# Position-bias rows written to memory once instead of 128 times, and another order of the first loads, in a four-layer encoder trunk

## Chip, cores and metric

One core of a Trainium2 chip runs the whole program. The metric is device microseconds of one execution, the median of the runs; three runs were taken of the kernel before.

## What is computed

Four post-norm layers run over 256 tokens of width 1024. Layers 0 and 3 mix tokens by differential attention with a shared relative-position bias, layer 1 by a gated linear recurrence, layer 2 by a short convolution. Each layer also attends to 256 memory tokens and ends with a gated feed-forward block. The part that the change touches is the bias of the attention layers, one number for each pair of positions and each of 6 heads, taken from a table of 32 buckets:

```python
bias = table[_t5_bucket(k_pos[None, :] - q_pos[:, None])].transpose(2, 0, 1)
logits = jnp.einsum('bqhmd,bkhmd->bmhqk', qb, k).astype(jnp.float32) + bias
probs = jax.nn.softmax(logits, axis=-1)
w = (probs[:, 0] - lam * probs[:, 1]).astype(v.dtype)
```

The bias depends on key position minus query position alone, so one row of 512 numbers for each head holds all of it.

## The kernel before

**Weights.** All weights lie in one stream in memory, cut into 404 units of 128 partitions x 4 KB (512 KB each), in the order of use. Unit u goes through four steps on four engines: SyncE issues its load into one of RAW = 5 buffers (line 473); ScalarE rounds it to a high part (line 784, "hi u" below); VectorE subtracts to get the low part (line 976, "lo u"); TensorE multiplies with both parts, three matmuls for each pair of tiles (lines 572 to 574, 584 to 588, 599 to 601). The high and low parts have SPLIT = 5 buffers of their own, so "hi u" waits until TensorE is done with unit u - 5 (`unit_done`), and the load of unit u waits for "lo" of unit u - 5 (`lo_ready`). A chunk is two units; a "half" is TensorE's work on one unit.

**Order.** `make_schedule` writes one list of items, and each engine walks it in order and does its own part of each item. At the head of the list stand: the turn (transposition) of the input tokens; chunk 0 (units 0 and 1, the query of the memory attention, "XQ"); `bias_rows`; the turn of the first 128 memory tokens ("turn mem 0"); chunk 1 (units 2 and 3, head 0's query and key, with "turn mem 1" between its halves); chunk 2 (units 4 and 5, keys of the memory, "KM"); chunk 3 (units 6 and 7, values of the memory) with the first memory logits "xlog 0" between its halves; then "xexp 0" (their exponentials on ScalarE, line 898) and `prepare` (small tables made ready on VectorE, which waits for all of `small_landed`); chunk 4 (units 8 and 9, head 1) with "xlog 1" between its halves; then "log 0", the first logits of the position-bias attention (line 668). While TensorE is on unit u, ScalarE and VectorE split unit u + 4. "log 0" uses the same PSUM banks as "xlog 0" and waits until "xexp 0" has read them.

**Bias.** TensorE multiplies the table with a one-hot matrix (line 649), ScalarE copies the resulting 6 x 512 rows from PSUM to `bias_rows` in SBUF (line 886, `rows_ready`). SyncE then writes them to `scratch` in memory once for each of 128 partitions (line 507, 1536 KB, `rows_out`), with a row pitch that makes a skewed reading possible, and reads them back skewed as `bias` (128 partitions x 6 heads x 384, line 491, 1152 KB, `bias_landed`), so that partition p holds the row shifted by p. This reading is done twice, for layer 0 and, later, for layer 3. VectorE adds the bias to the logits and takes the row maximum in one instruction (line 1177), 4 for each head.

**SyncE's queue.** All loads are issued by SyncE, one after the other, and a wait there holds all that stands behind it. The order at the start is: tokens, identity, units 0 to 2, one-hot matrix and table, memory tokens (`y_tok`, 1024 KB), units 3 and 4, eight small tables (the seven of `small[2:]` and `lam_w`), then units 5, 6, ... each after its `lo_ready`. The wait for `rows_ready` and the scratch write stand behind unit 9 (`u == RAW + 4`), the wait for `rows_out` and the bias load behind unit 13 (`u == RAW + 8`).

Of the kernel before, what the change touches and what calls it, by code (L numbers as in the profile page):

```python
# [25 lines left out]
P = 128  # L26
SEQ = 256
# [5 lines left out]
HEADS = MIX // P  # L33
# [4 lines left out]
HD = 64  # L38
# [9 lines left out]
RAW, SPLIT, AHEAD = 5, 5, 4  # L48
LEVELS = 8

ALU = mybir.AluOpType
ACT = mybir.ActivationFunctionType
F32 = mybir.dt.float32
# [127 lines left out]
def trunk_kernel(nc, stream, x, mem, rel_bias, ln, ln_cols, lam, subln, lower, hnorm, cconv, fconv,  # L181
# [38 lines left out]
    for pos, item in enumerate(items):  # L220
# [15 lines left out]
        if name == "hpv" or (name == "pv" and item[2] % 2 == 0):  # L236
            p = item[2] if name == "hpv" else item[2] // 2
# [6 lines left out]
    with ExitStack() as ctx:  # L244
        def sb(name, shape, dt=F32):
            return ctx.enter_context(nc.sbuf_tensor(name, shape, dt))

        def sem(name):
            return ctx.enter_context(nc.semaphore(name))
# [42 lines left out]
        row_max = sb("row_max", [P, 2, 4])  # L292
# [9 lines left out]
        with ExitStack() as place:  # L302
            def here(name, shape, dt=F32):
                return place.enter_context(nc.sbuf_tensor(name, shape, dt))
# [9 lines left out]
        with ExitStack() as place:  # L314
# [10 lines left out]
            bias = here("bias", [P, HEADS, 384])  # L325
            onehot = here("onehot", [NB, 512])
            table = here("table", [NB, HEADS])
            bias_rows = here("bias_rows", [HEADS, 512])
            masks_in = here("masks_in", [P, LEVELS, P])
            lam_w = here("lam_w", [P, 2, 4, HD])  # L330
# [26 lines left out]
        def head_sq(layer, p):  # L357
# [7 lines left out]
        table_landed, small_landed, bias_landed, rows_out = sem("table_landed"), sem("small_landed"), sem("bias_landed"), sem("rows_out")  # L365
# [22 lines left out]
        h_ready, prod_ready, gb_read = sem("h_ready"), sem("prod_ready"), sem("gb_read")  # L388
        dve_step, pool_step = sem("dve_step"), sem("pool_step")

        scratch = nc.dram_tensor("bias_scratch", [P, HEADS, 512], F32, kind="Internal").ap()
        out_dram = out.rearrange("b (t p) d -> p (b t) d", p=P)
        x_dram = x.rearrange("b (t p) d -> p (b t) d", p=P)
        mem_dram = mem.rearrange("b (t p) d -> p (b t) d", p=P)
        small = [(onehot, onehot_c), (table, rel_bias), (ln_col, ln_cols), (masks_in, masks_c), (fconv_w, fconv),
                 (cconv_w, cconv), (hnorm_w, hnorm), (subln_w, subln), (lower_w, lower)]
        SMALL = 16 * (len(small) - 2 + 1)

        def first_of(layer, roles):
            return next(c for c, ch in enumerate(chunks) if ch[2] == layer and ch[1] in roles)  # L400
# [58 lines left out]
        def side_bank(pos, k=0):  # L459
            return SIDE[side_ord[pos, k][0]]  # L460
# [4 lines left out]
        @block.sync  # L465
        def _(sp):
            for t in range(TT):
                sp.dma_start(x_tok[:, t], x_dram[:, t]).then_inc(x_landed[t], 16)
                if t == 0:
                    sp.dma_start(ident[:], ident_c).then_inc(ident_landed, 16)  # L470

            def load_unit(u):
                sp.dma_start(raw[:, u % RAW, :], stream[u // 2, :, (u % 2) * UNIT:(u % 2 + 1) * UNIT]).then_inc(
                    raw_landed[u % RAW], 16)

            load_unit(0)
            load_unit(1)
            load_unit(2)
            for dst, src in small[:2]:
                sp.dma_start(dst[:], src).then_inc(table_landed, 16)  # L480
            sp.dma_start(y_tok[:], mem_dram).then_inc(mem_landed, 16)
            for u in range(3, RAW):
                load_unit(u)
            for dst, src in small[2:]:
                sp.dma_start(dst[:], src).then_inc(small_landed, 16)
            sp.dma_start(lam_w[:], bass.AP(tensor=lam.tensor, offset=0, ap=[[0, P], [1, 2 * 4 * HD]])).then_inc(
                small_landed, 16)

            def load_bias():

                sp.dma_start(bias[:], bass.AP(tensor=scratch.tensor, offset=127,
                                              ap=[[HEADS * 512 - 1, P], [512, HEADS], [1, 384]])).then_inc(bias_landed, 16)

            for u in range(RAW, 2 * nchunks):
                c = u // 2
                sp.wait_ge(lo_ready, u - RAW + 1)
                load_unit(u)
                if u % 2 == 0 and c in load_gains:
                    m = load_gains[c]
                    if m >= 1:  # L500
                        sp.wait_ge(x_ready, TT * m)
                    sp.dma_start(gains[:], bass.AP(tensor=ln.tensor, offset=m * 2 * D,
                                                   ap=[[0, P], [1, 2 * D]])).then_inc(gains_landed, 16)
                if u == RAW + 4:

                    sp.wait_ge(rows_ready, 1)
                    sp.dma_start(scratch.rearrange("p h i -> h p i"),
                                 bias_rows[:].rearrange("h (one i) -> h one i", one=1).broadcast_to([HEADS, P, 512])).then_inc(rows_out, 16)
                if u == RAW + 8:
                    sp.wait_ge(rows_out, 16)  # L510
                    load_bias()
                if u == 2 * first_of(2, ("CG",)) + 16:
                    sp.wait_ge(x_ready, TT * 4)
                    load_bias()
            for t in range(TT):

                sp.wait_ge(*((x_ready, TT * (2 * DEPTH - 1) + 1) if t == 0 else (out_ready, 1)))
                sp.dma_start(out_dram[:, t], x_tok[:, t]).then_inc(out_landed, 16)
            sp.wait_ge(out_landed, 16 * TT)
# [441 lines left out]
        def _(dve):  # L961
# [3 lines left out]
            def link(ins):  # L965

                steps[0] += 1
                ins.then_inc(dve_step, 1)
                dve.wait_ge(dve_step, steps[0])
# [27 lines left out]
            def two(ap):  # L997
                return ap.rearrange("p (a s) -> p a s", a=2)
# [97 lines left out]
            for pos, item in enumerate(items):  # L1096
# [7 lines left out]
                elif name == "turn" and item[1] not in ("x", "mem"):  # L1104
                    m, t, n = item[1], item[2], ordinal[pos]
                    for b in range(2):
                        at = (slice(None), slice(4 * b, 4 * b + 4), slice(t * P, (t + 1) * P))
# [15 lines left out]
                elif name == "turn":  # L1123
                    what, t = item[1], item[2]
                    n = ordinal[pos]
                    hi, lo = (memT_hi, memT_lo) if what == "mem" else (xT_hi, xT_lo)
                    for b in range(2):
                        at = (slice(None), slice(4 * b, 4 * b + 4), slice(t * P, (t + 1) * P))
# [3 lines left out]
                elif name == "stats":  # L1132
# [4 lines left out]
                    for h in range(2):  # L1137
                        at = slice(h * 512, (h + 1) * 512)
# [25 lines left out]
                elif name in ("xlog", "log"):  # L1164
                    n = logit_ord[pos]
                    s = n % 2
                    dve.wait_ge(logits_done, n + 1)
                    if name == "xlog":
                        for i in range(2):
                            last = v.tensor_reduce(row_max[:, s, 2 * i:2 * i + 2], two(ACC[2 * s + i][:]), AX, ALU.max)  # L1170
                    else:
                        if n == head_logit[0] or n == head_logit[HEADS]:
                            dve.wait_ge(bias_landed, 16 if n == head_logit[0] else 32)
                        for i in range(2):
                            for t in range(TT):
                                j, at = 2 * i + t, (1 - t) * P
                                last = v.tensor_tensor_reduce(
                                    lg[:, s, i, t, :], ACC[2 * s + i][:, t * SEQ:(t + 1) * SEQ],
                                    bias[:, item[2], at:at + SEQ], 1.0, -3.0e38, ALU.add, ALU.max, row_max[:, s, j:j + 1])
                    link(last)  # L1180
                    v.tensor_scalar(neg_max[:, s, :], row_max[:, s, :], -1.0, None, ALU.mult).then_inc(max_ready, 1)
                elif name in ("xprob", "prob"):
                    n = prob_ord[pos]
                    s = n % 2
# [27 lines left out]
                elif name == "ms":  # L1212
                    p = item[2]
# [3 lines left out]
                elif name == "scale":  # L1217
                    layer, p = item[1:]
# [4 lines left out]
                    for i in range(2):  # L1223
                        s = slice(i * SEQ, (i + 1) * SEQ)
                        h = 2 * p + i
# [8 lines left out]
                elif name == "level":  # L1234
                    p, n = item[2], item[3]
# [3 lines left out]
                    if n < LEVELS:  # L1239
                        dst, src = DG[:, p].rearrange("p i k s -> p (i k s)"), side_bank(pos)[:]  # L1240
# [86 lines left out]
def shape_constants():  # L1327


    half, exact = NB // 2, NB // 4  # L1330
    rel = np.arange(-SEQ + 1, SEQ + 1)
    n = np.abs(rel)
    nf = np.maximum(n, 1).astype(np.float32)
    large = exact + (np.log(nf / np.float32(exact)) / np.float32(math.log(MAXD / exact))
                     * np.float32(half - exact)).astype(np.int32)
    bucket = np.where(rel > 0, half, 0) + np.where(n < exact, n, np.minimum(large, half - 1))
    onehot = (bucket[None, :] == np.arange(NB)[:, None]).astype(np.float32)
    s, t = np.arange(P)[:, None], np.arange(P)[None, :]
    masks = np.zeros((P, LEVELS, P), np.float32)
    masks[:, 0] = s == t  # L1340
    for level in range(1, LEVELS):
        b = 2 ** (level - 1)
        masks[:, level] = (s // (2 * b) == t // (2 * b)) & (s // b != t // b)
    return np.eye(P, dtype=np.float32), onehot, masks
# [29 lines left out]
```

## Time and profile before

| | us |
|---|---|
| median of 3 runs | 1437.44 |
| lowest and highest run | 1436.44, 1437.8 |
| span of the profiled execution | 1437.8 |
| TensorE busy in it | 1329.0 |
| VectorE busy | 1022.9 |
| ScalarE busy | 717.2 |

The span of the profiled execution equals the time of the highest of the runs, 0.36 us over the median. Times in the rows below are microseconds from the span's start. PE is TensorE, PEld its weight loads, ACT ScalarE, DVE VectorE, SPq the queue of SyncE. The granted clock of TensorE is given as a share of full speed: 1.00 is 2.4 GHz and 0.50 is 1.2 GHz.

### The profile page before, as it was taken

To read this page: it belongs to the slowest core of one execution; us is meant where nothing else is said; L and a number is where in the kernel's file an instruction comes from. 1 tells how busy PE (TensorE), PEld (TensorE's weight loads), DVE (VectorE), ACT (ScalarE), POOL (GpSimd) and SP (SyncE) were. 2 spreads that over 40 slices of the span, in tenths; PEclk is the share of its full clock that TensorE was granted. 3 is DMA by queue.
4 is the path that set the end of the run, shared out by engine and by line. 5 is a ranking of instruction groups with operands and counts; after the bars stand their busy time and mean duration, and the time that the engine had idled before them with its cause. 6 is when DMAs were issued, how large, how long until landed. Compare 5 with 4: busy or idle time off the path is not lost.

```text
span 1437.8 us, 23522 instructions
## 1 busy us (share of the span) xinstructions
PE 1329.0 (92%) x9366; PEld 1238.5 (86%) x9366; DVE 1022.9 (71%) x1536; ACT 717.2 (50%) x1147; POOL 150.5 (10%) x122
## 2 busy tenths in 40 slices
PE   7599899999799999799999899899998999699997
PEld 6489799999689998799998798899997998699996
DVE  4186777677859867877778677777678565777677
ACT  4185365555462233555554633655554763555552
POOL 0000300000304430300002002100003001300001
PEclk8789999999999999999999899899998999899999
DMA  7454265555352233365553374455553543265551
GB/s 255 112 202 130 89 202 189 193 190 180 108 183 90 90 103 132 126 227 183 189 186 132 132 231 140 161 205 182 188 188 109 199 133 118 89 233 177 187 191 47
DMA packets 64019, 230.09 MB, mean 160 GB/s; under 512 B 7431, under 2 KB 9223, under 8 KB 62887
## 3 DMA queue, kind: packets, MB, share of 16 engines
q1 hardware_dynamic: 63910, 228.60, 47.6%
q8 instruction: 74, 1.21, 0.3%
q14 instruction: 35, 0.28, 0.1%
HBM read 225.95 MB, written 2.62 MB: 159 GB/s over the span
## 4 chain that ended last, share of the span: by engine, by line
PE 67%; issue 18%; DVE 6%; DMA 4%; POOL 2%; ACT 2%; SPq 0%; POOLq 0%; DVEq 0%; ACTq 0%
PE proj L572 14%; PE proj L573 13%; PE proj L574 13%; PE acc L599 5%; PE acc L601 5%; PE acc L600 5%; DMA raw<-in_stream 4%; PE side L767 2%; PE proj L584 1%; DVE y_tok L1154 1%; PE proj L586 1%; PE proj L588 1%; POOL rstd L1267 1%; DVE w_lo L976 1%; PE acc L668 1%
## 5 line engine op out<-in xcount | busy, mean ns | idle before, releaser
L572 PE MATMUL proj<-xT_hi,w_hi 128*128 128x256 f32 x2000 | 579.8, 290 | 37.5 <-issue 33.0
L976 DVE TENSOR_TENSOR w_lo<-raw,w_hi 128x1024 fp32r<-128x1024 f32 x404 | 480.7, 1220 | 170.2 <-ACT w_hi L784 168.4
L784 ACT ACTIVATE w_hi<-raw 128x1024 fp32r<-128x1024 f32 x404 | 427.1, 1060 | 318.7 <-PE proj L574 144.8
L573 PE MATMUL proj<-xT_lo,w_hi 128*128 128x256 f32 x2000 | 574.2, 287 | 0.0
L574 PE MATMUL proj<-xT_hi,w_lo 128*128 128x256 f32 x2000 | 573.8, 287 | 0.0
L572 PEld LDWEIGHTS proj<-xT_hi,w_hi 128*128 128x128 f32 x2000 | 393.0, 196 | 46.3 <-issue 44.9
L573 PEld LDWEIGHTS proj<-xT_lo,w_hi 128*128 128x128 f32 x2000 | 392.8, 196 | 1.5
L574 PEld LDWEIGHTS proj<-xT_hi,w_lo 128*128 128x128 f32 x2000 | 392.2, 196 | 0.0
L989 DVE SCALAR_TENSOR_TENSOR cv<-hid,fconv_w,cv 128x255 f32<-128x255 f32 x176 | 77.4, 481 | 139.5 <-ACT cv L824 139.5
L601 PE MATMUL acc<-w_hi,gT_lo 128*128 128x512 f32 x352 | 139.0, 395 | 0.0
L600 PE MATMUL acc<-w_lo,gT_hi 128*128 128x512 f32 x352 | 139.0, 395 | 0.0
L599 PE MATMUL acc<-w_hi,gT_hi 128*128 128x512 f32 x352 | 139.0, 395 | 0.0
L815 ACT ACTIVATE hid<-proj 128x512 f32<-128x512 f32 x88 | 52.6, 598 | 149.3 <-PE proj L574 149.3
L1267 POOL TENSOR_TENSOR rstd<-var_eps,minus_half 128x1 f32<-128x1 f32 x16 | 16.2, 1015 | 911.6 <-DVE var_eps L1148 911.6
L601 PEld LDWEIGHTS acc<-w_hi,gT_lo 128*128 128x128 f32 x352 | 66.0, 187 | 16.1
L993 DVE SCALAR_TENSOR_TENSOR cv<-hid,fconv_w,cv 128x255 f32<-128x255 f32 x176 | 77.4, 481 | 3.1
L599 PEld LDWEIGHTS acc<-w_hi,gT_hi 128*128 128x128 f32 x352 | 66.2, 188 | 14.5
L600 PEld LDWEIGHTS acc<-w_lo,gT_hi 128*128 128x128 f32 x352 | 66.0, 187 | 14.4
L824 ACT ACTIVATE cv<-proj,fconv_w 128x256 f32<-128x256 f32 x176 | 73.4, 473 | 0.0
L868 ACT ACTIVATE xf<-side,ln_col 128x128 f32<-128x128 f32 x84 | 31.5, 455 | 61.7 <-DVE xT_lo L1121 47.2
L599 PE MATMUL acc<-w_hi,mixT_hi 128*128 128x512 f32 x128 | 52.0, 406 | 1.7 <-DVE mixT_lo L982 1.7
L601 PE MATMUL acc<-w_hi,mixT_lo 128*128 128x512 f32 x128 | 50.1, 391 | 0.0
(169 smaller groups left out, 1566.1 us busy)
## 6 DMA issues: line engine op xcount, KB each, us to landing
raw<-in_stream SPq DMA_DIRECT2D x404, 512.0 KB, 4.7
gains<-in_ln SPq DMA_DIRECT2D x8, 1024.0 KB, 8.5
bias<-bias_scratch SPq DMA_DIRECT2D x2, 1152.0 KB, 8.0
bias_scratch<-bias_rows SPq DMA_DIRECT2D x1, 1536.0 KB
x_tok<-in_x SPq DMA_DIRECT2D x2, 512.0 KB, 4.4
y_tok<-in_mem SPq DMA_DIRECT2D x1, 1024.0 KB, 10.1
out<-x_tok SPq DMA_DIRECT2D x2, 512.0 KB, 2.8
masks_in<-in_masks_c SPq DMA_DIRECT2D x1, 512.0 KB, 11.5
```

The source lines that it names most:

```text
L572: pe.matmul(bank, w_hi[:, slot, at], a_hi(k, every), start=(k == 0), stop=False)
L573: pe.matmul(bank, w_hi[:, slot, at], a_lo(k, every), start=False, stop=False)
L574: last = pe.matmul(bank, w_lo[:, slot, at], a_hi(k, every), start=False, stop=(k == KT - 1))
L599: pe.matmul(dst, b_hi(k, tok), w_hi[:, slot, at], start=begin, stop=False)
L600: pe.matmul(dst, b_hi(k, tok), w_lo[:, slot, at], start=False, stop=False)
L601: last = pe.matmul(dst, b_lo(k, tok), w_hi[:, slot, at], start=False, stop=end)
L784: nc.scalar.activation(w_hi[:, u % SPLIT, :], raw[:, u % RAW, :], ACT.Copy).then_inc(hi_ready, 1)
L815: nc.scalar.activation(hid[:, w], bank[:].rearrange("p (a s) -> p a s", a=2), ACT.Copy)
L824: last = nc.scalar.activation(cv[:, w, i, :], bank[:, i * SEQ:(i + 1) * SEQ], ACT.Copy, scale=fconv_w[:, layer, 1, first + i:first + i + 1])
L976: v.tensor_tensor(w_lo[:, u % SPLIT, :], raw[:, u % RAW, :], w_hi[:, u % SPLIT, :].bitcast(F32), ALU.subtract).then_inc(lo_ready, 1)
L989: last = v.scalar_tensor_tensor(dst[i][:, 1:SEQ], src[i][:, 0:SEQ - 1], weights(0, i), dst[i][:, 1:SEQ], ALU.mult, ALU.add)
L993: last = v.scalar_tensor_tensor(dst[i][:, 0:SEQ - 1], src[i][:, 1:SEQ], weights(2, i), dst[i][:, 0:SEQ - 1], ALU.mult, ALU.add)
```

## The change

The scratch in memory holds one copy of the 6 rows instead of 128. The one-hot matrix is reversed along the positions (on the host), so that the rows come out reversed; the load reads them with a pitch of one element from partition to partition, and line 1177 reads its 256 numbers of the bias backwards (step -1). The order of SyncE's issues is changed: units 0 to 3 stand ahead of the one-hot matrix and the table, unit 4 ahead of the memory tokens, and the eight small tables follow one by one behind the loads of units 5 to 12. The wait for `rows_ready` with the scratch write now stands behind unit 6, the wait for `rows_out` with the bias load behind unit 8.

```diff
-        scratch = nc.dram_tensor("bias_scratch", [P, HEADS, 512], F32, kind="Internal").ap()
+        scratch = nc.dram_tensor("bias_scratch", [HEADS, 512], F32, kind="Internal").ap()
...
-            load_unit(0)
-            load_unit(1)
-            load_unit(2)
+            for u in range(4):
+                load_unit(u)
             for dst, src in small[:2]:
                 sp.dma_start(dst[:], src).then_inc(table_landed, 16)
+            load_unit(4)
             sp.dma_start(y_tok[:], mem_dram).then_inc(mem_landed, 16)
-            for u in range(3, RAW):
-                load_unit(u)
-            for dst, src in small[2:]:
-                sp.dma_start(dst[:], src).then_inc(small_landed, 16)
-            sp.dma_start(lam_w[:], bass.AP(tensor=lam.tensor, offset=0, ap=[[0, P], [1, 2 * 4 * HD]])).then_inc(
-                small_landed, 16)
+
+            def load_small(n):
+                if n < len(small):
+                    dst, src = small[n]
+                    sp.dma_start(dst[:], src).then_inc(small_landed, 16)
+                elif n == len(small):
+                    sp.dma_start(lam_w[:], bass.AP(tensor=lam.tensor, offset=0, ap=[[0, P], [1, 2 * 4 * HD]])).then_inc(
+                        small_landed, 16)
 
             def load_bias():
 
-                sp.dma_start(bias[:], bass.AP(tensor=scratch.tensor, offset=127,
-                                              ap=[[HEADS * 512 - 1, P], [512, HEADS], [1, 384]])).then_inc(bias_landed, 16)
+                sp.dma_start(bias[:], bass.AP(tensor=scratch.tensor, offset=1,
+                                              ap=[[1, P], [512, HEADS], [1, 384]])).then_inc(bias_landed, 16)
 
             for u in range(RAW, 2 * nchunks):
                 c = u // 2
                 sp.wait_ge(lo_ready, u - RAW + 1)
                 load_unit(u)
+                load_small(2 + u - RAW)
...
-                if u == RAW + 4:
+                if u == RAW + 1:
 
                     sp.wait_ge(rows_ready, 1)
-                    sp.dma_start(scratch.rearrange("p h i -> h p i"),
-                                 bias_rows[:].rearrange("h (one i) -> h one i", one=1).broadcast_to([HEADS, P, 512])).then_inc(rows_out, 16)
-                if u == RAW + 8:
+                    sp.dma_start(scratch, bias_rows[:]).then_inc(rows_out, 16)
+                if u == RAW + 3:
                     sp.wait_ge(rows_out, 16)
                     load_bias()
...
-                                    bias[:, item[2], at:at + SEQ], 1.0, -3.0e38, ALU.add, ALU.max, row_max[:, s, j:j + 1])
+                                    bass.AP(tensor=bias, offset=item[2] * 384 + 383 - at, ap=[[HEADS * 384, P], [-1, SEQ]]), 1.0, -3.0e38, ALU.add, ALU.max, row_max[:, s, j:j + 1])
...
+    bucket = bucket[::-1]
     onehot = (bucket[None, :] == np.arange(NB)[:, None]).astype(np.float32)
```

## Rows read from the trace of the kernel before

**Rows 1.** Busy time by stretch: stretch, us, then engines; PEclk, DMA share, GB/s last.

```profile
54.20:74.40 20.20, 0.01 (x1) 0.02 (x1) 4.70 (x13) 4.53 (x11) 0.00 (x0) 0.55 0.46 127
74.40:80.30 5.90, 5.89 (x26) 5.15 (x27) 5.27 (x27) 4.44 (x10) 0.00 (x0) 0.51 0.94 340
80.30:130.00 49.70, 49.70 (x400) 45.71 (x398) 36.29 (x105) 37.16 (x95) 0.00 (x0) 1.00 0.45 151
```

**Rows 2.** TensorE in order of time: start, us, instruction group, idle before and releaser.

```profile
21.28 1.02 PE L649 MATMUL side<-onehot,table 32*6 32x512 f32 x2
25.17 1.61 PE L642 MATMUL side<-ident,y_tok 128*128 128x128 f32 x8 [2.87 <-ACT bias_rows L886]
30.50 1.03 PE L642 MATMUL side<-ident,y_tok 128*128 128x128 f32 x8
42.98 1.14 PE L657 MATMUL acc<-km,xq 64*128 64x256 f32 x8
...
74.41 2.08 PE L668 MATMUL acc<-qk 64*128 64x256 f32 x8 [20.20 <-ACT ex L898]
```

**Rows 3.** Waits from 40 to 75 us: us in total, times, longest.

```profile
ACT w_hi L784 <- DMA raw<-in_stream: 28.0, 2, 27.8
```

**Rows 4.** SyncE's queue in order of time: issues of loads and of the scratch write.

```profile
10.49 1.24 SPq L485 DMA_DIRECT2D lower_w<-in_lower  x1
11.76 1.09 SPq L486 DMA_DIRECT2D lam_w<-in_lam  x1
...
25.05 0.35 SPq L507 DMA_DIRECT2D bias_scratch<-bias_rows  x1
25.44 24.31 SPq L473 DMA_DIRECT2D raw<-in_stream  x4
67.32 0.38 SPq L491 DMA_DIRECT2D bias<-bias_scratch  x1
```

**Rows 5.** The weight load issued at 25.44 us alone: issue to landing.

```profile
DMA to landing us min/median/max: 43.1/43.1/43.1
```

**Rows 6.** The chain of work that ended last, in order of time, 80 to 100 us.

```profile
84.06 0.87 PE side L680 x8
84.93 1.07 PE acc L668 x8
...
91.95 1.02 PE side L700 x8
```

**Rows 7.** ScalarE in order of time.

```profile
23.01 1.06 ACT L784 ACTIVATE w_hi<-raw 128x1024 fp32r<-128x1024 f32 x1 [4.54 <-DMA raw<-in_stream]
...
24.45 0.57 ACT L886 ACTIVATE bias_rows<-side 6x512 f32<-6x512 f32 x1
...
40.21 0.60 ACT L799 ACTIVATE km<-proj 128x512 f32<-128x512 f32 x1 [1.76 <-PE proj L574]
```

**Rows 8.** Busy time by stretch, two idle times of TensorE later in the kernel.

```profile
466.60:467.80 1.20, 0.10 (x2) 0.04 (x1) 1.17 (x4) 0.00 (x0) 0.00 (x0) 1.00 0.00 0
467.80:475.00 7.20, 7.20 (x61) 7.03 (x62) 5.23 (x7) 2.94 (x5) 2.56 (x3) 1.00 0.24 76
...
411.00:414.80 3.80, 3.77 (x19) 3.77 (x20) 1.25 (x2) 3.80 (x8) 0.00 (x0) 0.55 0.41 138
```

**Rows 9.** DMA issues: count, KB each, median us from issue to landing.

```profile
raw<-in_stream SPq DMA_DIRECT2D x404, 512.0 KB, 4.7
...
bias<-bias_scratch SPq DMA_DIRECT2D x2, 1152.0 KB, 8.0
...
out<-x_tok SPq DMA_DIRECT2D x2, 512.0 KB, 2.8
...
lam_w<-in_lam SPq DMA_DIRECT2D x1, 256.0 KB, 10.0
...
lower_w<-in_lower SPq DMA_DIRECT2D x1, 24.0 KB, 9.3
```

**Rows 10.** Line 1177 in layer 0: ns min/median/max, first and last start.

```profile
L1177 DVE CUSTOM_DVE_ANT_0 lg<-acc,bias x24: 412/419/425, 81.1 to 119.5; 128x256 f32<-128x256 f32 x24
```

## The prediction

> **What bounds the kernel now.** I read first the busy time by stretch, to find where TensorE, busy for 1329.0 of 1437.8 us, is not. From 54.2 to 74.4 us it stands still for 20.20 us, then works at half clock (0.51) to 80.3, and from there to 130 it is busy in every microsecond at full clock while VectorE and ScalarE have a quarter of their time free [rows 1]. So outside the hole this stage is bound by TensorE, and the hole is the thing to explain. TensorE's own rows say that it stood before "log 0", released by the exponentials on ScalarE [rows 2]. The waits say what ScalarE stood for in the same stretch: 27.8 us at a stretch for a weight load [rows 3]. SyncE's queue says which: the load issued at 25.44, right behind the scratch write of 25.05 [rows 4], took 43.1 us to land [rows 5], where the median of the 404 takes 4.7 [rows 9]. It landed at 68.5; the wait for the scratch write ended at 67.32 [rows 4]. Loads are thus served in the order of issue, and unit 10 stood behind a write of 1536 KB that needed 67.32 - 25.05 = 42.3 us, 36 GB/s. All later units, "xexp 0" behind "hi 10" on ScalarE and "log 0" behind "xexp 0" followed.
>
> A smaller hole lies before it: TensorE ended the one-hot matmul at 22.30 and stood to 25.17 for ScalarE's copy of the bias rows [rows 2], which came at 24.45 because ScalarE had waited to 23.01 for unit 5 [rows 7], whose load stood behind the eight small tables.
>
> **Part 1: the small hole.** With the tables moved behind later units, unit 5 has 1133 KB less ahead of it. At 340 GB/s [rows 1] that is 3.3 us, so it lands by about 19.7 instead of 23.0 and "hi 5" (1.06 us) is over by 20.8, before TensorE ends chunk 0. Then the copy of the bias rows waits only for the matmul's end, 22.30, and starts at about 22.4 instead of 24.45 [rows 2, 7]: 2.05 us gained. If unit 5 came only 2.0 us earlier, 1.2 would be left. Units 3 and 4, now ahead of the memory tokens, come earlier too, but nothing waits for them; the memory tokens come later by two units, about 3 us at that rate, and are needed only at 23.1. Unit 0's place in the queue is unchanged, and so is the first matmul of chunk 0.
>
> **Part 2: the clock behind the small hole.** Behind the idle 2.87 us the work from 25.17 to 30.50, eight transposes and one half, took 5.33 us. At full clock eight transposes take 0.87 (84.06 to 84.93) and one set of logits with two halves takes 91.95 - 84.93 = 7.02, of which the logits are 1.07 [rows 6], so a half is 2.98 and the pair 3.85. The slow clock cost 5.33 - 3.85 = 1.48 us. The new idle time is 0.8 us (22.30 to 23.1). An idle time of about 1.1 us at 466.7 left the clock at 1.00, one of about 2.1 us before 411 was followed by 0.55 [rows 8]. The new one is nearer to the first, so I take the whole 1.48; the bounds are 0 and 1.48.
>
> **Part 3: the large hole.** The write shrinks from 128 copies to one, 12 KB. At the old write's rate that is 0.33 us of data; with the fixed part, the nearest write is that of the result, 2.8 us from issue to landing [rows 9]. Then unit 10 is no longer held. "log 0" starts where TensorE stopped, 20.20 us earlier [rows 2]. From "log 0" at 74.41 to the next transposes at 84.06 the logits and two halves took 9.65 us, where the same at full clock takes 7.02 [rows 2, 6]: 2.63 us of slow clock go too. Together 22.83 us. That nothing else holds TensorE there rests on its being busy without a gap from 80.3 to 130 when ScalarE and VectorE had just been set back [rows 1]; in the new order they are some 5 us further ahead at "log 0".
>
> **Part 4: what SyncE's queue now waits for.** The wait for `rows_ready` moves from behind unit 9 to behind unit 6 and ends at about 23.0; queued behind it are the write, units 7 and up, and the tables. The wait for `rows_out` stands behind unit 8 and holds the bias load and units 9 and up. In order: the write is issued at 23.0, unit 7 at 23.4 and lands at 27.6 to 28.1 (4.7 us at the most [rows 9]); "hi 7" wants it at about 29, since all of TensorE's dates come 3.5 us earlier by parts 1 and 2. Unit 8, behind a 264 KB table, lands at about 29.7, wanted at 31.5. `rows_out` is there at 23.0 + 2.8 = 25.8, the bias load is issued, and unit 9 behind it. The bias load's data begins when unit 8 is in, at 29.7, and unit 9 lands 1152 KB and 512 KB later. At 340 GB/s this is 3.4 + 1.5 us, so 34.6. **Its due date:** "hi 9" stands on ScalarE ahead of the copy of the memory keys, which "xlog 0" on TensorE needs, at 42.98 - 3.5 = 39.5. With 1.06 for "hi 9" and 0.60 for the copy [rows 7], unit 9 may land up to 37.8. So the load of the bias may take up to 6.6 us without cost. No row shows a load whose 128 partitions read overlapping rows of one 12 KB stretch. Bounds: spread over 1536 KB, the same 1152 KB take 8.0 us from issue to landing, fixed part included [rows 9], so about 3.4 of data. The other end is `lam_w`, 256 KB in which all partitions read the same 2 KB: it landed at 11.76 + 10.0 = 21.8, and the table ahead of it at 10.49 + 9.3 = 19.8 [rows 4, 9], 2.0 us, which for 1152 KB makes 9.0. I take some 4 to 6, nearer to the first, as the rows of a head are shifted and six stretches alternate: no cost. At 9.0 unit 9 lands at 40.2, 2.4 us late.
>
> The eight tables are all issued by unit 12, whose load waits for "lo 7", at about 32; the last lands near 39, and `prepare` wants it at about 43. The bias itself lands by 40 at the latest and is wanted by line 1177 at about 52. Both waits are covered, by TensorE's work on units 6 to 9.
>
> **Part 5: the backward reading.** Line 1177 keeps its count, 4 x 6 in each of two layers, and its shape, 0.419 us [rows 10]. No row shows a step of -1. I take no change; bounds are 0 and twice the time. Twice would add 24 x 0.42 = 10 us to VectorE's 36.3 in 49.7 us [rows 1], still under the stretch, so most is covered even then. A gain is not to be had, as the number of elements is the same. The Trainium skill, "VectorE: DVE Perf Modes", section "Mode 1× (REGULAR) — the baseline", says that the one-element-a-cycle mode that 4-byte data runs in "makes no assumptions" and takes any stride; by it the price is nil, and no row here shows it yet.
>
> **Sum.** 2.05 + 1.48 + 22.83 = 26.36 us. The profiled span 1437.8 becomes 1411.4; it lies 0.36 over the median, so 1411.1 is the forecast.
>
> **Rivals.** (a) A new wait in place of the old: the bias load is slow and unit 9 comes late. Speaks for it `lam_w`'s 2.0 us; against it the slack of 3.2 us. At 9.0 us of data: 2.4 us of idle and perhaps 1.5 of clock behind it, 1413.5 to 1415. At 11 us, 4.4 + 1.5, 1417. The Trainium skill, "DMA: Bandwidth & Descriptors", section "Latency and other measured facts", says that streams which step through memory in lockstep at some pitches fall to half, 103 GB/s at the worst; by it the load is an estimated 11 us, and no row of this case shows such a fall. (b) VectorE becomes the bound through the backward reading: with the double price exposed in one half of the 48 places, 10 us, 1421. Against it VectorE's free quarter. (c) Parts 1 or 2 fail, as the unit comes late or the clock falls all the same: 1412.5 to 1414.6. (d) Slower: the bias load crawls as the write did, at 36 GB/s, because all engines read one small stretch. It takes 32 us. In layer 0 it holds unit 9 for 25 us over its slack; in layer 3 the second load holds the weights behind it for 32 less the some 12 us that four split units ahead give, 20; with the clock some 48 in all against 26 gained: 1459. It decides from about 21 us on (55 GB/s). Against it: even `lam_w` got 130 GB/s. (e) The write of 12 KB is as slow as the old one, for a reason that is not its size: then unit 9 waits as unit 10 did, now at the earlier place, and the time is about 1437.
>
> **Chances.** Forecast 0.68 (1408.5 to 1412.5), (a) 0.14, (b) 0.04, (c) 0.08, (d) 0.03, (e) 0.02, 0.01 for faster still. The range 1408 to 1417 takes in the forecast, (c) and most of (a). About 0.2% is what a measurement of this kernel tells from no change; of the cases, (d) and a bad end of (e) are slower, a good end of (e) is the same: faster 0.95, same 0.015, slower 0.035.
>
> **What would show it.** Unit 10's load lands within 10 us; TensorE has no idle time over 1 us between 23.2 and 130 and its clock stays at 1.00 from about 19 on; ScalarE's copy of the bias rows starts near 22.4; "log 0" starts near 50.7; line 1177 stays at 0.42 us; the bias load takes under 10 us from issue to landing. The prediction is wrong if ScalarE waits for a weight load between 34 and 45 us, or if line 1177 is longer and TensorE waits for the exponentials in layers 0 and 3.

## The result, and the profile after

The changed kernel takes 1414.16 us (median of 4 runs, 1413.79 to 1415.31) against 1437.62 for the kernel before (4 runs): ratio 0.983, interval 0.9813 to 0.9846. Beside later experiments it was measured twice more: 1416.99 against 1441.85 and 1414.49 against 1438.21, ratios 0.9826 (0.9812 to 0.9841) and 0.9829 (0.9815 to 0.9842). The gain is 23.5 to 24.9 us; 26.4 were forecast, 1411.1 us, with a range of 1408 to 1417.

The new lines of the kernel have numbers up to 3 higher (line 668 is 671, 1177 is 1180). Busy time by stretch in the changed kernel, columns as in [rows 1]:

```profile
22.70:50.20 27.50, 27.50 (x226) 26.38 (x227) 17.28 (x44) 13.88 (x27) 0.00 (x0) 1.00 0.85 296
50.20:60.00 9.80, 9.80 (x80) 8.91 (x81) 6.00 (x19) 9.80 (x30) 0.00 (x0) 1.00 0.44 158
```

The hole of [rows 1] is gone: from 22.7 to 60 TensorE is busy in every microsecond and the clock stays at 1.00. TensorE in order of time, where [rows 2] had 21.28, 25.17, 30.50, 42.98 and 74.41; the last row is the kernel before, its transposes behind "log 0":

```profile
20.88 1.02 PE L652 MATMUL side<-onehot,table 32*6 32x512 f32 x2
22.67 1.06 PE L645 MATMUL side<-ident,y_tok 128*128 128x128 f32 x8 [0.77 <-ACT bias_rows L889]
26.45 1.03 PE L645 MATMUL side<-ident,y_tok 128*128 128x128 f32 x8
38.92 1.14 PE L660 MATMUL acc<-km,xq 64*128 64x256 f32 x8
...
50.08 1.14 PE L671 MATMUL acc<-qk 64*128 64x256 f32 x8
57.01 1.03 PE L683 MATMUL side<-ident,prob 128*128 128x128 f32 x8
...
83.89 1.03 PE L680 MATMUL side<-ident,prob 128*128 128x128 f32 x8
```

The idle time before the memory tokens' transposes is 0.77 us instead of 2.87. "log 0" starts at 50.08, without a wait, instead of 74.41. ScalarE, against [rows 7]:

```profile
19.01 1.06 ACT L787 ACTIVATE w_hi<-raw 128x1024 fp32r<-128x1024 f32 x1 [2.81 <-DMA raw<-in_stream]
...
21.94 0.59 ACT L889 ACTIVATE bias_rows<-side 6x512 f32<-6x512 f32 x1 [0.35 <-PE side L652]
...
34.78 1.06 ACT L787 ACTIVATE w_hi<-raw 128x1024 fp32r<-128x1024 f32 x1 [2.79 <-DMA raw<-in_stream]
36.15 0.60 ACT L802 ACTIVATE km<-proj 128x512 f32<-128x512 f32 x1 [0.31 <-PE proj L577]
```

Unit 5 came 4 us earlier, so the bias rows now wait for the matmul and for nothing else. ScalarE does wait 2.79 us for unit 9 behind the bias load, but the copy of the memory keys behind it still waits for TensorE (0.31), so that wait costs nothing. SyncE's queue, the scratch write, the bias load and unit 9, and below it the loads of unit 9 and of unit 10 (issued at 27.58), each alone:

```profile
22.55 0.33 SPq L511 DMA_DIRECT2D bias_scratch<-bias_rows  x1
...
25.73 0.43 SPq L494 DMA_DIRECT2D bias<-bias_scratch  x1
26.20 0.54 SPq L473 DMA_DIRECT2D raw<-in_stream  x1
...
DMA to landing us min/median/max: 8.6/8.6/8.6
DMA to landing us min/median/max: 8.6/8.6/8.6
```

Line 1180 in layers 0 and 3, and the two bias loads from issue to landing, against [rows 10] and [rows 9]:

```profile
L1180 DVE CUSTOM_DVE_ANT_0 lg<-acc,bias x24: 417/420/425, 51.4 to 92.6; 128x256 f32<-128x256 f32 x24
DMA to landing us min/median/max: 7.8/7.8/7.8
...
L1180 DVE CUSTOM_DVE_ANT_0 lg<-acc,bias x24: 418/420/425, 1109.2 to 1150.0; 128x256 f32<-128x256 f32 x24
DMA to landing us min/median/max: 8.2/8.2/8.2
```

The backward reading costs nothing (0.420 us against 0.419), as the Trainium skill has it ("VectorE: DVE Perf Modes", section "Mode 1× (REGULAR) — the baseline"). Nor is the reading of overlapping rows slow: 7.8 and 8.2 us, where rows spread over 1536 KB took 8.0. The fall of lockstep streams of which the same skill tells ("DMA: Bandwidth & Descriptors", section "Latency and other measured facts") does not show at this pitch of one element; the page calls its cause an inference.

A mark that every kernel here has is GpSimd's reciprocal root in the first norm, the end of layer 0's attention: first the kernel before, then the changed one.

```profile
163.42 0.55 POOL L1267 TENSOR_TENSOR rstd<-var_eps,minus_half 128x1 f32<-128x1 f32 x1 [9.69 <-DVE var_eps L1148]
...
136.53 0.55 POOL L1270 TENSOR_TENSOR rstd<-var_eps,minus_half 128x1 f32<-128x1 f32 x1 [9.68 <-DVE var_eps L1151]
```

Up to here 26.89 us are gained. Of these 0.40 stand ahead of the one-hot matmul (20.88 against 21.28), and where that matmul stands differs by as much between executions of the changed kernel: 20.88, 20.77 and 20.35 in its three profiles. From the one-hot matmul to the mark the kernel before takes 163.42 - 21.28 = 142.14 us and the changed one 136.53 - 20.88 = 115.65, so 26.49 are gained there. This distance is 115.65 and 115.66 us in the other two profiles of the changed kernel, so it tells the kernels below apart more finely than the whole time. The spans differ by 1437.8 - 1412.6 = 25.2: 1.7 of the 26.89 were lost behind the mark.

### The profile page after: what moved, and what is told of

It reads as the page before. It is cut to its first block, busy times and chain, and to the rows that moved or that the text cites. A ratio compares the mean times of both kernels' runs of the same rounds, so it can differ in the third digit from the quotient of the medians.

```text
span 1412.6 us, 23522 instructions
## 1 busy us (share of the span) xinstructions
PE 1326.7 (94%) x9366; PEld 1236.5 (88%) x9366; DVE 1022.2 (72%) x1536; ACT 717.2 (51%) x1147; POOL 152.3 (11%) x122
## 3 DMA queue, kind: packets, MB, share of 16 engines
HBM read 225.95 MB, written 1.06 MB: 161 GB/s over the span
## 4 chain that ended last, share of the span: by engine, by line
PE 71%; issue 18%; DVE 6%; POOL 2%; ACT 2%; DMA 1%; SPq 0%; POOLq 0%; DVEq 0%; ACTq 0%
PE proj L575 15%; PE proj L576 14%; PE proj L577 14%; PE acc L602 5%; PE acc L604 5%; PE acc L603 5%; PE side L770 2%; PE proj L587 1%; PE proj L589 1%; PE proj L591 1%; DVE y_tok L1157 1%; POOL rstd L1270 1%; DVE w_lo L979 1%; PE acc L671 1%; DVE stats L1148 1%
## 5 line engine op out<-in xcount | busy, mean ns | idle before, releaser
L1270 POOL TENSOR_TENSOR rstd<-var_eps,minus_half 128x1 f32<-128x1 f32 x16 | 16.2, 1015 | 912.0 <-DVE var_eps L1151 912.0
```

## The experiments

The theory: two terms add. The long write held the weights behind it (part 3), the tables held unit 5 (parts 1 and 2), and the earlier waits of part 4 cost nothing while unit 9 comes before its due date. The rivals: the short write alone is the gain; the earlier places are part of it; DMA bandwidth and not the order of service was the cause; every microsecond ahead of unit 9 counts. Each run's time stands beside runs of the kernel before on the same chip.

**One copy, old order.** The short write, the new load and the backward reading, but SyncE's order and both places as before.

```diff
-            for u in range(4):
-                load_unit(u)
+            load_unit(0)
+            load_unit(1)
+            load_unit(2)
...
-                load_small(2 + u - RAW)
...
-                if u == RAW + 1:
+                if u == RAW + 4:
...
-                if u == RAW + 3:
+                if u == RAW + 8:
```

> One copy of the rows, the one-pitch load and the backward reading as in the changed kernel, but SyncE's order and the places of both waits as before. Theory (the write and the order of the loads are two terms that add): the small hole and the slow clock behind it come back, 2.5 + 1.5 us, so 1418 us against 1414.2 of the changed kernel and 1437.6 of before; ScalarE's copy of the bias rows starts near 24.5, the clock is 0.5 behind it, TensorE has no idle time before log 0. Rival (the whole gain is the shorter write, the order is worth nothing): 1414 us.

It took 1418.28 against 1439.67, ratio 0.9853 (0.9838 to 0.9867): 21.4 us of gain. TensorE behind the bias rows, the busy time there and from there to 130 us, and the mark of the first norm:

```profile
24.66 1.73 PE L642 MATMUL side<-ident,y_tok 128*128 128x128 f32 x7 [3.14 <-ACT bias_rows L886]
...
24.60:28.20 3.60, 3.54 (x20) 3.57 (x20) 1.61 (x3) 2.14 (x3) 0.00 (x0) 0.60 0.78 259
28.20:130.00 101.80, 101.61 (x765) 93.18 (x764) 65.41 (x168) 60.61 (x135) 3.80 (x3) 1.00 0.45 153
...
139.85 0.55 POOL L1267 TENSOR_TENSOR rstd<-var_eps,minus_half 128x1 f32<-128x1 f32 x1 [9.69 <-DVE var_eps L1148]
```

The small hole (3.14 us) and the slow clock (0.60) are back, the large hole is not: behind 28.2 TensorE is busy for 101.61 of 101.80 us. From its one-hot matmul at 20.51 to the mark the kernel takes 119.34 us, 3.7 more than the changed one, where parts 1 and 2 made 3.5. So with the short write the order of the loads is worth its two terms, and the short write the rest.

**The order only.** The old write, its load and both places, with the new order of the loads.

```diff
-            load_unit(0)
-            load_unit(1)
-            load_unit(2)
+            for u in range(4):
+                load_unit(u)
             for dst, src in small[:2]:
                 sp.dma_start(dst[:], src).then_inc(table_landed, 16)
+            load_unit(4)
...
+                load_small(2 + u - RAW)
```

> The new order of the first loads and of the small tables, but the 1536 KB write, its load and both waits where they were before. Theory (weights queue behind the write, so what the order gains ahead of it is swallowed by the wait, but the write itself starts 2.5 us earlier): unit 10 lands 42 us after the write's issue at about 22.6, so near 66; time 1435 us; the clock gain of 1.5 us is not to be seen. Rival (the terms add): 1433.5 us. Rival (order worth nothing without the short write): 1437.5 us.

1437.62 against 1439.67, ratio 0.9986 (0.9977 to 0.9996): 2.05 us, where some 2.6 were expected. SyncE's queue with the landing of unit 10 (issued at 22.45), TensorE at "log 0", and the mark:

```profile
22.07 0.34 SPq L510 DMA_DIRECT2D bias_scratch<-bias_rows  x1
22.45 14.45 SPq L473 DMA_DIRECT2D raw<-in_stream  x1
...
55.94 3.80 SPq L473 DMA_DIRECT2D raw<-in_stream  x1
...
DMA to landing us min/median/max: 43.6/43.6/43.6
...
71.86 1.23 PE L671 MATMUL acc<-qk 64*128 64x256 f32 x4 [22.19 <-ACT ex L901]
...
159.77 0.55 POOL L1270 TENSOR_TENSOR rstd<-var_eps,minus_half 128x1 f32<-128x1 f32 x1 [9.70 <-DVE var_eps L1151]
```

The hole is there, 2 us longer (22.19) since TensorE came to it earlier, and it ends 2.55 us earlier (71.86 against 74.41) because the write started 3 us earlier. What the order gains ahead of a wait goes into the wait. At the mark 3.65 are gained, 1.1 more, as from "log 0" to the next transposes (80.23) this profile took 8.37 us, the one of before 9.48: its half clock behind the hole was shorter.

**The old write at the new places.** The kernel of the last experiment with `RAW + 4` and `RAW + 8` changed to `RAW + 1` and `RAW + 3`.

```diff
-                if u == RAW + 4:
+                if u == RAW + 1:
...
-                if u == RAW + 8:
+                if u == RAW + 3:
```

> The new order and the new, earlier places of both waits, but the 1536 KB write and its load as before. Theory: the write now stands ahead of unit 7 and the bias load ahead of unit 9, so unit 9 lands near 72 instead of 35 us, the memory keys' copy and xlog 0 behind it come near 74 instead of 39 us, with slow clock behind: 1414 + 35 + 2.6 = about 1452 us, slower than before. Rival (an earlier write always gives an earlier end): 1433 to 1435 us.

1451.89 against 1439.67, ratio 1.0092 (1.0076 to 1.0109): 12.2 us slower. TensorE's two waits:

```profile
68.21 0.55 PE L587 MATMUL proj<-w_hi,memT_hi 128*128 128x256 f32 x1 [31.66 <-ACT qk L809]
...
75.47 0.49 PE L660 MATMUL acc<-km,xq 64*128 64x256 f32 x2 [1.97 <-ACT km L802]
```

The size was near what was expected, the place half so: most of the wait came before "xlog 0", at chunk 3, which wants the PSUM bank that ScalarE empties only after "hi 7" (31.66 us), and 1.97 more came at "xlog 0". With the long write the earlier places do harm.

**The changed kernel with the old places.** The same two lines changed back in the changed kernel.

```diff
-                if u == RAW + 1:
+                if u == RAW + 4:
...
-                if u == RAW + 3:
+                if u == RAW + 8:
```

> The changed kernel with the two waits (and with them the small write and the bias load) back behind units 9 and 13. Theory: both are covered, the bias is wanted only at 51 us and lands near 43; unit 9 lands some 5 us earlier, which nothing needs: 1414 us, within 1. Rival (the earlier places are a part of the gain): 1416 us or more, with a wait before line 1180 at log 0.

1412.98 against 1439.67, ratio 0.9817 (0.9803 to 0.9832). The bias load, issued at 32.88, and the mark:

```profile
DMA to landing us min/median/max: 6.8/6.8/6.8
...
135.74 0.55 POOL L1270 TENSOR_TENSOR rstd<-var_eps,minus_half 128x1 f32<-128x1 f32 x1 [9.67 <-DVE var_eps L1151]
```

The bias lands at 39.7 and is wanted at 51. From the one-hot matmul at 20.11 to the mark the kernel takes 115.63 us, the changed one 115.65, so the earlier places neither gain nor cost. The changed kernel was not run on the same chip, so whether 1412.98 is better as a whole is not told. The kernel with one copy and the old order did run on this chip, and only the order of the loads sets it apart from this one: 1418.28 against 1412.98, 5.3 us, of which 119.34 - 115.63 = 3.7 lie between the one-hot matmul and the mark. With the old write the same order gave 2.05 us. The order and the short write thus do not simply add: what the order gains counts in full only when the wait behind it is gone.

**The write on another queue.** The kernel before; ScalarE issues the 1536 KB write on its own DMA queue.

```diff
                     nc.scalar.activation(bias_rows[:], side_bank(pos)[0:HEADS, :], ACT.Copy).then_inc(
                         rows_ready, 1)
+                    act.wait_ge(rows_ready, 1)
+                    act.dma_start(scratch.rearrange("p h i -> h p i"),
+                                  bias_rows[:].rearrange("h (one i) -> h one i", one=1).broadcast_to([HEADS, P, 512])).then_inc(rows_out, 16)
...
-                if u == RAW + 4:
-
-                    sp.wait_ge(rows_ready, 1)
-                    sp.dma_start(scratch.rearrange("p h i -> h p i"),
-                                 bias_rows[:].rearrange("h (one i) -> h one i", one=1).broadcast_to([HEADS, P, 512])).then_inc(rows_out, 16)
```

> The kernel before, with one change: the 1536 KB write is issued by ScalarE on its own DMA queue instead of SyncE. Its size, the bias load, the waits and SyncE's order stay. Theory (units 10 and up stood in line behind the write in SyncE's queue): unit 10 lands within 15 us of its issue instead of 43, TensorE's idle 20 us before log 0 at 54 go, and the next thing that is late is the bias itself, which still needs the 42 us: SyncE waits for the write behind unit 13 as before, so unit 14 and the bias land near 77 to 82 and TensorE stands at about 69 us, before the first memory values, for some 15 to 20 us: 3 to 8 us faster than before. Rival (the write takes the DMA engines, the queue is no matter): unit 10 near 67 us, idle at 54, time of before.

1433.36 against 1441.85, ratio 0.9952 (0.9933 to 0.997): 8.5 us faster, a little more than expected. The landing of unit 10, the busy time from 25.4 us, the waits from 40 to 90, and TensorE at the memory values:

```profile
DMA to landing us min/median/max: 16.2/16.2/16.2
...
25.40:69.30 43.90, 43.90 (x344) 41.72 (x344) 18.90 (x46) 18.29 (x40) 0.00 (x0) 0.96 0.40 91
...
ACT w_hi L779 <- DMA raw<-in_stream: 20.9, 3, 18.1
DVE lg L1175 <- DMA bias<-bias_scratch: 18.7, 1, 18.7
...
82.23 0.70 PE L695 MATMUL side<-xprobT,vm 128*64 128x256 f32 x2 [12.89 <-ACT xprobT L916]
```

With nothing else changed, unit 10 lands after 16.2 us and not 43.1, and TensorE is busy without a gap to 69.3. So it was mainly the place in SyncE's queue that held the weights. The 16.2 us are still twice the 8.6 of the changed kernel; whether that is the write's share of the DMA engines no run tells apart. Two other waits come out that the first had hidden: VectorE waits 18.7 us for the bias itself, and unit 14 stands behind SyncE's wait for the write (18.1 us on ScalarE). TensorE stands 12.89 us at 69 to 82. The write had two roads to TensorE; of the runs here only those with the short write close both.

**How late may unit 9 come?** In the changed kernel one, and then three, loads of 768 KB that nobody reads stand between the bias load and unit 9; the count that `prepare` waits for goes up with them.

```diff
                     load_bias()
+                    for dst in (KE[0], KE[1], v_tok):
+                        flat = dst[:] if len(dst.shape) == 2 else dst[:].rearrange("p h s -> p (h s)")
+                        sp.dma_start(flat, stream[0, :, 0:HEADS * SEQ]).then_inc(small_landed, 16)
```

> The changed kernel with one more load of 768 KB (weights, never used) between the bias load and unit 9, to test how late unit 9 may come. Theory (due date: unit 9 is wanted on ScalarE in time for the memory keys' copy ahead of xlog 0 at 38.9, so it may land up to 37.2; it landed at 34.8): unit 9 lands 2 us later, near 36.8, ScalarE waits for it longer and TensorE does not: the time of the changed kernel, within 1 us. Rival (every microsecond in front of unit 9 counts): 2 us more.

> The changed kernel with three more loads of 768 KB (never used) between the bias load and unit 9. Theory (due date 37.2): unit 9 lands near 40.6 to 41, TensorE stands before xlog 0 for 3 to 4 us, then perhaps 1.5 us of slow clock: 3 to 5 us more than the changed kernel. Rival (units 6 to 8, already split, cover it all): no more than the changed kernel. Rival (it all counts): 6 us more.

With one load 1414.74, with three 1421.12, the changed kernel beside them 1416.99 and the kernel before 1441.85. First the kernel with one load, ScalarE's "hi 9" and the mark; then that with three, "hi 9", TensorE at "xlog 0", the stretch behind and the mark:

```profile
37.36 1.06 ACT L790 ACTIVATE w_hi<-raw 128x1024 fp32r<-128x1024 f32 x1 [5.37 <-DMA raw<-in_stream]
...
136.65 0.55 POOL L1273 TENSOR_TENSOR rstd<-var_eps,minus_half 128x1 f32<-128x1 f32 x1 [9.69 <-DVE var_eps L1154]
```

```profile
40.43 1.06 ACT L790 ACTIVATE w_hi<-raw 128x1024 fp32r<-128x1024 f32 x1 [8.56 <-DMA raw<-in_stream]
...
42.12 0.49 PE L663 MATMUL acc<-km,xq 64*128 64x256 f32 x2 [3.25 <-ACT km L805]
...
42.10:52.00 9.90, 9.88 (x79) 9.07 (x80) 9.01 (x34) 6.53 (x15) 0.00 (x0) 1.00 0.96 347
...
139.74 0.55 POOL L1273 TENSOR_TENSOR rstd<-var_eps,minus_half 128x1 f32<-128x1 f32 x1 [9.69 <-DVE var_eps L1154]
```

The due date of unit 9 is 37.2 ("xlog 0" at 38.9, less the key copy of 0.60 and the split of 1.06). Unit 9 at 37.36 costs 0.1 us: from the one-hot matmul at 20.88 to the mark it is 115.77. Unit 9 at 40.4 is 3.2 past the date, TensorE waits 3.25, and the mark is 3.3 later. The due date holds to about a tenth of a microsecond, and up to it the wait on ScalarE (5.37 us) is free. No clock was lost behind the 3.25 us in this execution. The whole times tell less: one load more came out 2.3 us under the changed kernel and three 4.1 over it. The execution profiled with three took 1417.21, the others 1420.6 to 1422.32; what those lost beyond the wait no row shows.

**What is left at the start.** Two edits on the kernel with the old places: the turn of the second token half ahead of unit 0's split, and then also three matmuls on zeros behind it, to keep TensorE at work where it idles for 3.8 us before chunk 0.

```diff
-    split_units(0)
     items.append(("turn", "x", 1))
+    split_units(0)
...
+                    if what == "x" and t == TT - 1:
+                        for _ in range(3):
+                            pe.matmul(ACC[0][:], xf[:, 0, 0:P], xf[:, 0, :], start=True, stop=True)
```

> What is left at the start: the changed kernel with the waits in their old places, and the turn of the second half of the tokens put ahead of unit 0's split in the item list. Theory (chunk 0 waits for the last low part of the tokens, which stands behind hi 0 and lo 0 on ScalarE and VectorE): chunk 0 starts near 12.0 to 12.3 instead of 12.7 to 13.1 us, 0.8 us gained at the first norm, hardly to be told in the whole time. Rival (unit 0's low part is then as late): nothing gained.

> The kernel of the run beside this, with three more matmuls on zeros, never read, behind the turn of the tokens, where TensorE idles for 3 to 4 us ahead of chunk 0. Theory (the idle time is followed by half clock through most of chunk 0, which then takes 7.8 us where two halves at full clock take 6.0): the clock stays at 1.00 through chunk 0, some 2 us gained at the first norm. Rival (the clock falls for another reason, or the extra matmuls end later than the tokens are ready): nothing, or a loss under 1 us.

1413.77 and 1412.33 us, the changed kernel beside them 1414.49 and the kernel before 1438.21; ratios to before 0.9828 (0.9814 to 0.9841), 0.9818 (0.9805 to 0.9831) and 0.9829 (0.9815 to 0.9842). None can be told from the others. First the start of chunk 0 with the turn alone. Then the kernel with the extra matmuls, TensorE at the end of chunk 0, ScalarE there, the busy time of chunk 0 and behind the next idle time, and its mark; last the changed kernel's mark on this chip:

```profile
12.06 0.58 PE L575 MATMUL proj<-xT_hi,w_hi 128*128 128x256 f32 x1 [2.94 <-DVE w_lo L979]
...
17.89 1.02 PE L655 MATMUL side<-onehot,table 32*6 32x512 f32 x2
20.61 0.44 PE L645 MATMUL side<-ident,y_tok 128*128 128x128 f32 x1 [1.70 <-ACT bias_rows L892]
...
18.45 1.06 ACT L790 ACTIVATE w_hi<-raw 128x1024 fp32r<-128x1024 f32 x1 [2.83 <-DMA raw<-in_stream]
...
12.00:18.00 6.00, 6.00 (x49) 5.84 (x50) 4.63 (x4) 2.66 (x3) 0.00 (x0) 1.00 1.02 387
...
20.60:24.00 3.40, 3.39 (x16) 3.40 (x17) 1.55 (x3) 2.02 (x3) 0.00 (x0) 0.50 1.04 391
...
135.99 0.55 POOL L1273 TENSOR_TENSOR rstd<-var_eps,minus_half 128x1 f32<-128x1 f32 x1 [9.66 <-DVE var_eps L1154]
```

```profile
136.01 0.55 POOL L1270 TENSOR_TENSOR rstd<-var_eps,minus_half 128x1 f32<-128x1 f32 x1 [9.68 <-DVE var_eps L1151]
```

With the turn alone chunk 0 started where it was expected, at 12.06, 0.6 earlier than with the old places alone (12.68), and the expected 0.8 us did not come: its matmuls ran at half clock to 17.0 instead of 16.0, the one-hot matmul stands at 20.18 against 20.11, and the mark at 135.83 against 135.74. With the extra matmuls the clock did stay at 1.00 through chunk 0, which ended 3 us earlier (17.89). Then TensorE stood 1.70 us for the bias rows, since "hi 5" waits for unit 5 until 18.45, and behind that the clock was 0.50. The whole gain went back into this wait and the slow clock behind it, and the mark is where it was (135.99 against 136.01). As the DMA share is 1.02, the start now seems bound by the loads ahead of unit 5; no run moved them further.

**The changed kernel again.** It ran beside both last groups.

> The changed kernel once more, beside these on one chip. All theories: about 25 to 26 us under the kernel before of the same chip; the first attention layer ends as in its first profile, the rest of the span moves by 1 to 2 us from run to run with where the clock falls.

> The changed kernel beside these two on one chip, to compare with. All theories: 23 to 26 us under the kernel before; 137 us at the first norm's reciprocal root.

Its marks are 136.53, 136.42 and 136.01 in the three profiles, its spans 1412.6, 1415.5 and 1411.7. From the mark to the end it took 1276.1, 1279.1 and 1275.7 us; the kernel before took 1437.8 - 163.42 = 1274.4 in its one profile, and the slowest experiment, the old write at the new places, 1447.9 - 174.57 = 1273.3. The same work behind the mark thus differs by up to 6 us between profiles, and by 3.4 between those of the changed kernel.

## Why the prediction was right, and where it was off

**Part 1** was right: 2.05 us forecast for the bias rows, 24.45 to 21.94 = 2.51 measured, 0.40 of which is the earlier one-hot matmul.

**Part 2** was right in size: from the first to the second transposes 3.78 us (22.67 to 26.45) against 5.33, 1.55 gained, 1.48 forecast. Its reason, by the nearest idle time, is weaker than it read: 3.25 us of idle left the clock at 1.00 in one run, and 1.70 us was followed by 0.50 in another.

**Part 3** was right. Unit 10 landed 8.6 us after its issue, "log 0" started at 50.08 and the next transposes stand at 57.01 instead of 83.89, 26.88 us earlier; the three parts made 26.36. The 84.06 of the prediction comes from the chain of [rows 6], which dates them 0.17 later than the rows in order of time from which its 74.41 was taken, so its 2.63 us of slow clock were 2.46. The run with the write on another queue shows the cause, the order of service; that with one copy alone shows the size.

**Part 4** was right, and its due date was measured: 37.2 where the text had 37.8, which leaves 6.0 us for the data of the load where it had 6.6. Unit 9 landed at 34.8, forecast 34.6. Rival (a) needs a slower load than there is. One bound was misread: the 4.7 us "at the most" for a load is the median of [rows 9], and unit 8 took 6.0, unit 7 ahead of it 4.1. One sign was too strict: ScalarE did wait for a weight load up to 34.78, inside the 34 to 45 us that were to prove the prediction wrong, and nothing was lost, as the due date allows it.

**Part 5** was right. Rivals (b), (d) and (e) fall with line 1180's 0.420 us, the load's 7.8 us and the write's end before 25.73.

**What was off** is the step from the sum to the time. The sum, 26.36, was right to 0.13 us between the one-hot matmul and the mark (26.49). The median gained 23.5, and 1414.16 lies outside the 1408.5 to 1412.5 of the main case. It lies where rivals (a) and (c) had been priced, and neither of them happened: it is luck that the range, widened for them, took in this time and, just, the 1416.99 measured later.

Two things make up the difference of 26.89 and 23.5. First, the prediction compared unlike times. It took the span, 1437.8, as the execution's time, 0.36 over the median. In every run where both stand, the time is 1.8 us over the span (1414.36 and 1412.6; 1417.61 and 1415.8), so the profiled execution of before is estimated at 1439.6, 2.2 over the median then known, and the profiled one of the changed kernel is 0.2 over its own. A gain read from the spans, 25.2, is so 1.7 more than that of the medians, 23.5. The slip alone leaves the forecast at 1411.1, since the median less 26.36 is the same sum; but it hid that the one profile was of a long execution. Where that execution lost its 2 us no row shows. The 33 runs of before, in four groups, have medians of 1437.62 to 1441.85.

Second, 1.7 us were lost behind the mark. The prediction had no term for that part. It is not line 1180: from the last norm of layer 2 to the first of layer 3, which holds layer 3's attention, it takes 1219.02 - 1092.80 = 126.22 us before and 1193.91 - 1067.76 = 126.15 after. Nor is it the second bias load: that is issued in layer 2 (at 836.8 in the kernel before), and there the changed kernel won 1.8 us. The loss, 3.6 us, lies from the mark to the end of layer 1. Why, in work that the change does not touch, stays open; the executions of the changed kernel differ there by 3.4 us among themselves.

## What to carry to other kernels

A long transfer on a queue is priced twice: by what waits for its data, and by what stands behind it in the queue; a trace names only the later of the two. Give each load behind such a wait a due date, worked out from the engine that needs it in order, and what comes before that date is free; the date can be measured by adding loads until the first engine waits. And time gained ahead of a wait that does not move goes into the wait, as the order alone in part, and the warm start in whole, showed.

## What the runs showed of the hardware

The write of 1536 KB from 6 partitions took 42.3 us (25.05 to 67.32), 36 GB/s over all. It did not run evenly: 50 GB/s moved with a DMA share of 0.35 in an early stretch, 25 with 0.23 in a late one. Three stretches of the kernel before, columns as in [rows 1]:

```profile
30.00:35.00 5.00, 5.00 (x45) 5.00 (x44) 2.51 (x3) 2.58 (x6) 0.00 (x0) 1.00 0.35 50
40.00:45.00 5.00, 5.00 (x42) 4.50 (x41) 0.00 (x0) 0.60 (x1) 0.00 (x0) 1.00 0.69 160
55.00:60.00 5.00, 0.00 (x0) 0.00 (x0) 0.00 (x0) 0.00 (x0) 0.00 (x0) 0.63 0.23 25
```

The Trainium skill ("DMA: Bandwidth & Descriptors", section "Why a DMA increments its semaphore by 16 and not by 1") says that a transfer is spread over as many engines, up to 16, as divide the outermost size of both its sides, here six. The shares fit that: 0.35 is 5.6 of 16 engines, 0.23 is 3.7. Why the rate halves no run here tells. In the middle stretch 160 GB/s moved, far more than the write's own rate, while no weight load landed between 40 and 67 us: the loads behind the write seem to have moved much of their data and still not to have landed until it was done.

Behind such a write even the issue of a load held SyncE: 14.45 us for one load and 3.8 for a later one (rows of the order only), where 0.33 is usual. And TensorE's clock does not follow the length of one idle time: 1.70 us was followed by 1.2 GHz, 3.25 us was not.
